# A first token mixer whose pool and convolution groups are normalised, turned and multiplied out ahead of its gating group

## The reference

```python
def token_mixer(h, w_in, pool_w, pool_scale, sgu_ln_g, sgu_ln_b, sgu_w, sgu_b, conv_w, group_g, w_out):
    p = h @ w_in                                   # 1024 -> 2048 columns
    a, u, v, gb, gc, xc = jnp.split(p, list(SPLITS), axis=-1)   # 256, 512, 512, 256, 256, 256
    y_a = pool_mixer(a, pool_w, pool_scale)        # running means over 2, 4, 8, 16 tokens, a small product, a scale
    y_b = sgu_mixer(u, v, sgu_ln_g, sgu_ln_b, sgu_w, sgu_b)     # u * (w_s @ layernorm(v) + b)
    y_c = short_conv_mixer(gb, gc, xc, conv_w)     # gb * conv3(gc * xc)
    y = jnp.concatenate([
        rmsnorm(y_a, group_g[:D_POOL]),
        rmsnorm(y_b, group_g[D_POOL:D_POOL + D_SGU]),
        rmsnorm(y_c, group_g[D_POOL + D_SGU:]),
    ], axis=-1)
    return y @ w_out

for l in range(2):                                 # first block
    x = x + token_mixer(rmsnorm(x, norm1_g[l]), ...)
    x = x + (swiglu(...) if l == 0 else moe_ffn(...))
```

## Time and profile before

| | |
|---|---|
| median of 3 runs | 2629.82 us (2627.33 to 2630.14) |
| the profiled execution | 2627.75 us |
| its span | 2626.0 us |
| granted TensorE clock, mean | 0.958 |
| PE busy | 2480.6 us (94%) |
| DVE busy | 1898.3 us (72%) |
| ACT busy | 1453.6 us (55%) |
| first mix1 stage, pieces begin / last rows begin | 37.21 / 121.93 us |
| second mix1 stage, pieces begin | 374.24 us |

### The profile page before, as it was taken

How to read it: one execution, slowest core, us unless ns; L and a number is a source line. 1 busy time by engine, 2 the same in 40 slices (tenths; PEclk the granted TensorE clock), 3 DMA queues, 4 the chain that set the end, 5 groups by cost and what they waited for, 6 DMA issues and landing times.

```text
span 2626.0 us, 39723 instructions
## 1 busy us (share of the span) xinstructions
PE 2480.6 (94%) x14992; PEld 2200.3 (84%) x14992; DVE 1898.3 (72%) x2061; ACT 1453.6 (55%) x1598; POOL 25.8 (1%) x47
## 2 busy tenths in 40 slices
PE   5799998799999999999999979998999999989998
PEld 5788887799999999999999968886788788867887
DVE  4676666588888888888888876668476676684665
ACT  3354443476767676767676754444444544544543
POOL 3000000000000000000000000000000000000000
PEclk8999999799999999999999989998799999996999
DMA  5455543398989898989898955542255555431552
GB/s 194 147 182 182 189 161 129 121 359 325 360 324 360 323 362 323 359 326 359 326 359 326 359 196 191 183 144 102 81 179 190 177 183 187 155 119 51 181 186 95
DMA packets 83809, 594.35 MB, mean 226 GB/s; under 512 B 9861, under 2 KB 10183, under 8 KB 12567
## 3 DMA queue, kind: packets, MB, share of 16 engines
q1 hardware_dynamic: 81216, 587.76, 62.5%
q0 software_dynamic: 1936, 4.44, 0.5%
q10 hardware_dynamic: 582, 1.16, 0.1%
HBM read 592.27 MB, written 1.05 MB: 226 GB/s over the span
## 4 chain that ended last, share of the span: by engine, by line
PE 87%; DVE 8%; ACT 2%; issue 1%; DMA 1%; ACTq 0%; DVEq 0%
PE banks L911 16%; PE banks L964 9%; PE banks L966 8%; PE banks L900 8%; PE banks L970 8%; PE banks L901 8%; PE banks L902 8%; PE banks L913 8%; DVE lo L1463 2%; PE banks L1187 2%; PE banks L940 2%; PE banks L1067 1%; DVE xhl L1540 1%; PE banks L998 1%; DMA stage_rows<-in_sgu_b 1%
## 5 line engine op out<-in xcount | busy, mean ns | idle before, releaser
L1463 DVE TENSOR_TENSOR lo<-raw,hi 128x2048 fp32r<-128x2048 f32 x550 | 1254.6, 2289 | 273.0 <-ACT hi L507 272.1
L507 ACT CAST hi<-raw 128x2048 fp32r<-128x2048 f32 x550 | 1049.8, 1909 | 232.3 <-PE banks L970 125.7
L911 PE MATMUL banks<-xhl,hi 128*128 128x512 f32 x1776 | 629.1, 398 | 1.2 <-DVE gsum L1494 1.2
L900 PE MATMUL banks<-hi,xhl 128*128 128x256 f32 x1952 | 566.7, 290 | 10.1 <-DVE xhl L1540 7.6
L901 PE MATMUL banks<-lo,xhl 128*128 128x256 f32 x1952 | 554.8, 284 | 0.0
L902 PE MATMUL banks<-hi,xhl 128*128 128x256 f32 x1952 | 554.8, 284 | 0.0
L913 PE MATMUL banks<-xhl,lo 128*128 128x256 f32 x1776 | 498.5, 281 | 0.0
L911 PEld LDWEIGHTS banks<-xhl,hi 128*128 128x128 f32 x1776 | 333.6, 188 | 83.7 <-DVE lo L1463 1.6
L900 PEld LDWEIGHTS banks<-hi,xhl 128*128 128x128 f32 x1952 | 376.2, 193 | 22.6 <-issue 15.7
L901 PEld LDWEIGHTS banks<-lo,xhl 128*128 128x128 f32 x1952 | 376.9, 193 | 2.6
L902 PEld LDWEIGHTS banks<-hi,xhl 128*128 128x128 f32 x1952 | 376.3, 193 | 0.0
(11 more groups left out here) (346 smaller groups left out, 2415.1 us busy)
## 6 DMA issues: line engine op xcount, KB each, us to landing
raw<-in_moe_w_gate SPq DMA_DIRECT2D x112, 1024.0 KB, 4.9
raw<-in_moe_w_up SPq DMA_DIRECT2D x112, 1024.0 KB, 4.9
raw<-in_moe_w_down SPq DMA_DIRECT2D x112, 1024.0 KB, 4.9
raw<-in_ffn_w_gate SPq DMA_DIRECT2D x58, 1024.0 KB, 4.8
raw<-in_ffn_w_up SPq DMA_DIRECT2D x58, 1024.0 KB, 4.8
raw<-in_ffn_w_down SPq DMA_DIRECT2D x58, 1024.0 KB, 4.8
raw<-in_mix_pieces SPq DMA_DIRECT2D x46, 1024.0 KB, 4.8
raw<-in_mix_pieces SPq DMA_DIRECT2D x2, 768.0 KB, 4.1
```

Of the source, the lines that this page charges most:

```text
L507: nc.scalar.copy(hi[:, hslot(S, c), 0:n], raw[:, c % RING, 0:n]).then_inc(S.hi_done, 1)
L900: pe.matmul(o, xh[:, x0 + k, tk], hi[:, hr, wgt], start=(first and n == 0), stop=False)
L911: pe.matmul(bank[b + s][:, :], hi[:, hr, a:a + P], xhl[:, k, :], start=(k == 0), stop=False, skip_group_check=True)
L1463: v.tensor_tensor(lo[:, c % RING, 0:n], raw[:, c % RING, 0:n], hi[:, hslot(S, c), 0:n].bitcast(F32), ALU.subtract).then_inc(S.lo_done, 1)
```

## The change

The pieces come in another order: a, gc, xc, gb, v, v, u, u, and the rows of `w_out` in the order pool, convolution, gating, gating (`MIX1_COLS`, `MIX1_ROWS`). DVE does the pool sums after `lo` B+3, the convolution after `lo` B+4, and `y1` of both groups after `lo` B+5; PE does the pool products after its third piece and the transposes of the convolution after its fourth. The norm of these two groups (the new `group_norm` and `squares`) and their four chunks (`EDGES`) go first: PE turns them after its sixth piece, and they are rounded into a new tile `yahl`. The statistics of v follow after that, then `vn`, and the gating products after the eighth piece. Then the product with the pool rows runs, then the gating chunks (`MIDDLE`) are turned, and the other three row pieces follow. PSUM banks and the columns of the small statistics tiles are dealt out anew.

```diff
-MIX1_COLS = (768, 1024, 0, 1536, 1792, 1280, 256, 512)
+MIX1_COLS = (0, 1536, 1792, 1280, 768, 1024, 256, 512)
+MIX1_ROWS = (0, 768, 256, 512)
...
+        yahl = s1("yahl", [P, 4, 2 * T], F32R)
+        yah, yal = yahl[:, :, 0:T], yahl[:, :, T:2 * T]
...
-        MIX1_BANKS = (0, 1, 6, 7, 2, 3, 4, 5)
+        MIX1_BANKS = (6, 7, 2, 3, 0, 1, 6, 7)
+        EDGES, MIDDLE = (0, 1, 6, 7), (2, 3, 4, 5)
-        Y_BANKS = (0, 1, 6, 7)
+        Y_BANKS = (4, 0, 1, 5)
... ACT
+            squares(((0, 0, DP), (2, DP + DS, D)), 1)
+            act.wait_ge(ev("y_var"), 2 * l + 1)
+            nc.scalar.activation(by_group(std)[:, :, ::2], by_group(var)[:, :, ::2], ACT.Sqrt).then_inc(ev("y_std"), 1)
+            act_hi(act, main, B + 7, 0)
+            act.wait_ge(ev("v_var"), l + 1)
+            nc.scalar.activation(std[:, 2:4], var[:, 2:4], ACT.Sqrt).then_inc(ev("v_std"), 1)
+            act_hi(act, main, B + 8, 0)
+            turned_y(lambda k: yah[:, k if k < 2 else k - 4, :], EDGES, 0)
             for i in range(2):
+                act.wait_ge(main.multiplied, B + 7 + i)
...
+            squares(((1, DP, DP + DS),), 2)
...
+            turned_y(lambda k: xh[:, k, :], MIDDLE, 2)
             act_hi(act, main, B + 11, 0)
... PE
-                if m in (2, 3, 4):
+                if m < 3:
                     pe_cols(pe, main, n, 0, bk, T).then_inc(main.multiplied, 1)
                 else:
+                    if m == 6:
+                        pe.wait_ge(ev("y_raw"), 2 * l + 1)
                     pe.wait_ge(main.lo_done, split_no(main, n) + 1)
                     pe_toks(pe, main, n, (bk, bk), FW).then_inc(main.multiplied, 1)
+                if m == 0:
+                    pe_turn_r(pe, st)
+                if m == 2:
+                    pe.wait_ge(ev("pool_in"), l + 1)
+                    pe.wait_ge(ev("poolw_in"), 64)
... (the four pool products)
+                if m == 3:
+                    pe.wait_ge(ev("conv_in"), l + 1)
... (the four transposes)
+                if m == 5:
+                    pe.wait_ge(ev("y_ready"), 2 * l + 1)
+                    pe_turn(pe, y1, Y_BANKS, EDGES, ev("y_turned"))
             pe.wait_ge(ev("vn_out"), 2 * (l + 1))
... (the eight gating products)
+            pe.wait_ge(ev("yl_out"), 8 * l + 4)
+            pe_rows(pe, main, B + 8, 0, yah[:, 0:2, :], yal[:, 0:2, :], TT, first=True)
+            pe.wait_ge(ev("y_ready"), 2 * (l + 1))
+            pe_turn(pe, y1, Y_BANKS, MIDDLE, ev("y_turned"))
+            pe_rows(pe, main, B + 9, 0, yah[:, 2:4, :], yal[:, 2:4, :], TT)
             pe.wait_ge(ev("yl_out"), 8 * (l + 1))
+            pe_rows(pe, main, B + 10, 0, xh[:, 2:4, :], xl[:, 2:4, :], TT)
+            pe_last_rows(pe, st, B + 11, xh[:, 4:6, :], xl[:, 4:6, :])
... POOL
-            pool.wait_ge(ev("y_raw"), 1)
+            pool.wait_ge(ev("y_raw"), 2)
... DVE
+                lo_piece(main, B + 2, 0)
+                lo_piece(main, B + 3, 0)
+                dve.wait_ge(main.multiplied, B + 1)
... (the pool sums, unchanged, up to pool_in)
+                lo_piece(main, B + 4, 0)
+                dve.wait_ge(main.multiplied, B + 3)
... (the convolution, unchanged, up to conv_in)
+                lo_piece(main, B + 5, 0)
... (y1 of the pool and convolution groups, then_inc y_raw)
+                lo_piece(main, B + 6, 0)
+                group_norm(((0, 0, DP), (2, DP + DS, D)), slice(0, 3, 2), 6 * l + 4, 1)
+                dve.wait_ge(main.multiplied, B + 6)
... (the statistics of v, up to v_var)
+                lo_piece(main, B + 7, 0)
... (vn, up to vn_out)
+                rest_y(lambda k: yal[:, k if k < 2 else k - 4, :], lambda k: yah[:, k if k < 2 else k - 4, :], EDGES, 0)
+                lo_piece(main, B + 8, 0)
+                lo_piece(main, B + 9, 0)
                 dve.wait_ge(ev("sgu_out"), 2 * (l + 1))
                 dve.wait_ge(ev("u_out"), 4 * (l + 1))
... (y1 of the gating group, then_inc y_raw)
+                group_norm(((1, DP, DP + DS),), 1, 6 * l + 6, 2)
+                lo_piece(main, B + 10, 0)
+                rest_y(lambda k: xl[:, k, :], lambda k: xh[:, k, :], MIDDLE, 4)
                 lo_piece(main, B + 11, 0)
```

More of the change, by code:

```diff
@@ L681, in act_mix1 @@
                 act_hi(act, main, B + m, 0)
[L682 to L687, removed]
+            act.wait_ge(main.multiplied, B + 4)
             act.wait_ge(rt_done, st["M"] + 1)
@@ L691, in act_mix1, with squares @@
                                      scale=rstd[:, t:t + 1]).then_inc(ev("gb_out"), 1)
+            act_hi(act, main, B + 6, 0)
+            def squares(groups, n):
+                act.wait_ge(ev("y_raw"), 2 * l + n)
+                for t in range(TT):
+                    for g, c0, c1 in groups:
+                        nc.scalar.activation(xn[:, t, c0:c1], y1[:, t, c0:c1], ACT.Square,
+                                             accum_out=ssq[:, 8 + 3 * t + g:9 + 3 * t + g]).then_inc(ev("y_sq"), 1)
@@ new lines, in turned_y @@
+            def turned_y(dst, chunks, n):
+                for i, k in enumerate(chunks):
+                    act.wait_ge(ev("y_turned"), 4 * l + n + i // 2 + 1)
+                    nc.scalar.activation(dst(k), bank[Y_BANKS[k // 2]][:, k % 2 * T:(k % 2 + 1) * T], ACT.Copy,
+                                         scale=col(("group", l), k)).then_inc(ev("yh_out"), 1)
+            squares(((0, 0, DP), (2, DP + DS, D)), 1)
+            act.wait_ge(ev("y_var"), 2 * l + 1)
+            nc.scalar.activation(by_group(std)[:, :, ::2], by_group(var)[:, :, ::2], ACT.Sqrt).then_inc(ev("y_std"), 1)
@@ L704, in act_mix1 @@
[L704 to L708, removed]
+                act_hi(act, main, B + 9 + i, 0)
+            squares(((1, DP, DP + DS),), 2)
+            act.wait_ge(ev("y_var"), 2 * l + 2)
@@ L1143, in pe_mix1 @@
                 n, bk = B + m, MIX1_BANKS[m]
[L1144 to L1147, removed]
-                if m in (2, 3, 4):
+                if m < 3:
                     pe_cols(pe, main, n, 0, bk, T).then_inc(main.multiplied, 1)
                 else:
+                    if m == 6:
+                        pe.wait_ge(ev("y_raw"), 2 * l + 1)
                     pe.wait_ge(main.lo_done, split_no(main, n) + 1)
                     pe_toks(pe, main, n, (bk, bk), FW).then_inc(main.multiplied, 1)
+                if m == 0:
[3 more added lines that the diff above has]
+                    pe.wait_ge(ev("poolw_in"), 64)
+                    for t in range(TT):
+                        for c in range(2):
+                            mm = pe.matmul(bank[6][:, t * 256 + c * P:t * 256 + c * P + P], dT[:, c, t * P:t * P + P],
+                                           poolw[:, l, c, :], start=True, stop=True)
+                    mm.then_inc(ev("pool_out"), 1)
+                if m == 3:
+                    pe.wait_ge(ev("conv_in"), l + 1)
+                    for t in range(TT):
+                        for c in range(2):
+                            mm = pe.transpose(bank[7][:, t * 256 + c * P:t * 256 + c * P + P],
+                                              zc[:, c, t * P:t * P + P], ident[:, :])
+                    mm.then_inc(ev("conv_out"), 1)
+                if m == 5:
+                    pe.wait_ge(ev("y_ready"), 2 * l + 1)
+                    pe_turn(pe, y1, Y_BANKS, EDGES, ev("y_turned"))
             pe.wait_ge(ev("vn_out"), 2 * (l + 1))
@@ L1685, in mix1 @@
                 mark(ev("conv_in"))
[L1686 to L1694, removed]
+                lo_piece(main, B + 5, 0)
+                if l == 0:
+                    dve.wait_ge(ev("small_in"), 16 * N_SMALL)
+                else:
+                    dve.wait_ge(ev("small1_in"), 48)
                 dve.wait_ge(ev("pool_out"), l + 1)
@@ L1702, in mix1 @@
                 ins.then_inc(ev("y_raw"), 1)
[L1703 to L1709, removed]
-                link(v.reciprocal(rstd[:, 2:8], std[:, 2:8]))
@@ new lines, in mix1, with group_norm @@
+                sums, vars_ = by_group(ssq), by_group(var)
+                def group_norm(groups, own, squares, n):
+                    dve.wait_ge(ev("y_sq"), squares)
+                    for g, c0, c1 in groups:
+                        ins = v.tensor_scalar(vars_[:, :, g], sums[:, :, g], 1.0 / (c1 - c0), EPS, ALU.mult, ALU.add)
+                    ins.then_inc(ev("y_var"), 1)
+                    dve.wait_ge(ev("y_std"), 2 * l + n)
+                    link(v.reciprocal(by_group(rstd)[:, :, own], by_group(std)[:, :, own]))
+                    for t in range(TT):
+                        for g, c0, c1 in groups:
+                            ins = v.tensor_scalar(y1[:, t, c0:c1], y1[:, t, c0:c1],
+                                                  rstd[:, 8 + 3 * t + g:9 + 3 * t + g], None, ALU.mult)
+                    ins.then_inc(ev("y_ready"), 1)
@@ new lines, in mix1 @@
+                for t in range(TT):
+                    for b in range(2):
```

(25 more changed lines are left out.)

94 lines of the change are left out of this document (19 added, 75 removed).

## The result

The changed kernel takes 2600.27 us (median of 4 runs, 2598.87 to 2601.27) against 2629.98 us in the same session (2627.33 to 2630.64). The ratio is 0.9887, with a 95% interval of 0.9872 to 0.9903: 29.7 us, 1.1% faster. Forecast were 2602.5 and a range of 2596 to 2611. A second session gave 2601.09 against 2630.27, ratio 0.9885 (0.9869 to 0.9902). Between the two profiled executions the difference is smaller, 26.5 us.

What follows compares the result with a forecast made beforehand. PE was taken as the bound, with only idle time and clock to gain. Time without a piece falls from 19.65 to 6.0 us a stage, 27.2 in all, giving 2602.5 us, range 2596 to 2611.

Steps and rivals of the forecast that it cites:

- The bound: PE, busy 94% of the span; with no matmul removed, only its idle time and the clock could yield a gain.
- Time without a piece: Time per stage when PE multiplies no input or row piece: from 19.65 us to 6.0.
- the prediction's bill: PE's time between input and row pieces before the change, listed as products, transposes and idle time: 19.65 us in total.
- the sum: Gain of 13.6 us a stage, 27.2 over both, taken from the kernel before.
- PE's small groups: Work on PE between pieces: pool products 0.90, convolution transposes 0.45, gating products 1.78, eight transposes 0.9 us.
- The 1.1 us of idle time: PE's remaining wait before turning the gating chunks: DVE's chain of 20.8 us against PE's work of 19.7.
- The waits of the first phase: PE's waits for `pool_in`, `conv_in` and the first `y_ready`, with slack of 0.2, 0.7 and 4.6 us.
- DVE's chain: Work from the end of the sixth piece to the scaled gating group, 20.8 us, which PE must wait for.
- Rival 1, the clock: Clock falls at the new pause in one or both stages: 3 to 7.8 us back, 2605.5 to 2610; chance 0.14.
- the step by which I set the rule of the Trainium skill aside: Transposes keep the clock up, read from its rise around 103 us; so nothing taken for the 7.8 us.
- Rivals 2 to 4: Gain part lost to new waits (2610, 0.08); half clock between input pieces (2640, 0.02); hole hidden otherwise (2629.8, 0.02).

Runs made afterwards that it cites:

- second run of the changed kernel: The changed kernel itself, unaltered, run once more on the chip of the later variants: 2601.09 us.
- the experiment with three additions: Changed kernel with three unused 128x512 additions on DVE ahead of the gating `y1` in each stage: 2604.69 us.
- the moved `lo` pieces: Kernel before, with `lo` B+9 moved behind `y1` and `lo` B+10 behind the scaling on DVE: 2627.38 us against 2630.27.
- the single norm: Changed kernel with one norm for all three groups at the end, all 16 transposes together and the row pieces behind them: 2616.70 us.
- the split row piece: Changed kernel with the second turn in the middle of row piece B+9 instead of ahead of it: 2597.25 us.
- the row piece behind the turn: Changed kernel with the pool rows (piece B+8) multiplied behind the turn of the gating chunks, not ahead of it: 2614.58 us.

## Why the prediction was right

**The bound.** What the change could gain stood at one place of each stage, as the prediction says, and nearly all of it was gained. Time without a piece in the first stage: forecast 6.0, measured 0.81 + 0.36 + 0.79 + 1.71 + 0.86 + 0.85 = 5.4, from the starts in the timeline above. Of the 14.3 us that went there, 12.0 are idle time (10.85 and 1.84, now 0.69) and 2.0 the sixteen transposes, which no longer run at half clock. (The single terms of the prediction's bill add up to 19.50; its total of 19.65 is taken from starts and is right.)

**The terms of the sum.** Each of PE's small groups was 0.05 to 0.11 us cheaper than I took it. The 1.1 us of idle time was 0.86. Against that stand two terms that I did not have, 0.4 each: the three row pieces take 16.8 us, not 16.45 (5.67, then 11.16 for two), 0.3 of it because the two that read the new tile `yahl` run slower (last section), and the input pieces up to the gating product 49.0, not 48.6, because after each group between them the next matmul starts 0.08 later, and the first piece ran 0.2 longer. So the first stage gained 13.49 against 13.6.

**The second stage** gained 15.07. 1.4 of the 1.5 above the sum lie in its first piece: it ran at half clock until 380.3 before and until 363.9 after, that is for 6.1 and 2.9 us. The second run of the changed kernel shows that the change has no part in it: there the piece was at half clock for 6.15 us, as before, and the stage took 75.59, a gain of 13.63 us against 13.6 forecast. The window of that first piece, in the second run's trace (columns as in the earlier trace rows):

```profile
361.30:367.45 6.15, 6.15 (x29) 6.15 (x30) 2.87 (x6) 3.05 (x5) 0.00 (x0) 0.50 0.00 0
```

Startup and what comes after the mixers gave back 2.1 (0.28 and 1.8), which leaves 26.5 in the span, 0.7 less than forecast. The medians differ by more, 29.7 us, and the four runs of the changed kernel fall in two pairs: 2598.87 and 2599.28 with a mean granted clock of 0.968, 2601.25 and 2601.27 with 0.963. That the median came out 2.2 us below the forecast is of this size: luck with the clock and not a term of the sum.

**The waits of the first phase** were reckoned at 0.2, 0.7 and 4.6 us of slack, and none showed. Measured from the end of DVE's work to the end of PE's piece, it was 0.3, 0.9 and 5.0. Moving one `lo` piece ahead of the pool sums turned the 0.2 into 4.5 us of idle time and 11.8 us of time, so these were the right places to watch.

**DVE's chain** is what binds now: 20.6 us measured for 20.8, and the experiment with three additions gives 2.16 us for 2.13.

**Rival 1, the clock.** It did not fall; nor did it after a pause of 2.85 us before the same transposes; with 4.53 among the pieces, and with 6.28 and 7.21 before the turn, it did. But the step by which I set the rule of the Trainium skill aside was weaker than I wrote. I read from the kernel before that sixteen transposes had raised the clock, so transposes count. With the moved `lo` pieces the same sixteen transposes ran from 97.35, with the same pause behind them, and the clock did not rise until 108.8, six microseconds into the rows, and in the second stage 3.2 us into them. After the single norm's sixteen, it rose at 100.8, 0.6 us into the rows. That transposes alone can be followed by a rise stands (the kernel before, both stages); that they reliably bring it does not. What the Trainium skill states in "TensorE: Matmul & The Clock Gate", Part 4: PE-mode transpose, that transposes don't count as busy for the clock, is contradicted by the first and agrees with the second, and what decides between them stays open. For the sum it made no difference: behind a pause of 0.86 us the clock stayed at 1.00 in both stages, and in the variant with 2.85 us too.

**Rivals 2 to 4.** No gain was lost in a new wait beyond the 0.86; no half clock among the pieces; nothing else had hidden the hole.

## What to carry to other kernels

Look for independent groups that share one norm, one turn and one product: finish those whose inputs come first, so that their share of the product stands ready for the pause which the last group's chain makes. The early norm by itself gave 0.65 us of the stage, and 8.3 with the row piece under the chain: what pays is matrix work placed where PE would wait. And a shorter pause is worth its length only if the clock agrees: 1.87 us less of it bought nothing in one stage of the kernel before, as the rows then began at half clock, and 0.4 us in the other.

## What the runs showed of the hardware that was not expected

The row matmuls run at two paces at full clock. The timeline of PE in the changed kernel around 104 us:

```profile
103.70 0.40 PE L982 MATMUL banks<-hi,xhl 128*128 128x512 f32 x1
103.94 0.39 PE L984 MATMUL banks<-lo,xhl 128*128 128x512 f32 x1
...
104.85 0.39 PE L984 MATMUL banks<-lo,xhl 128*128 128x512 f32 x1
105.08 0.39 PE L982 MATMUL banks<-hi,xhl 128*128 128x512 f32 x1
```

From start to start it is 0.233 us a matmul within the row pieces from 90.49 to 104.2, and 0.227 from 104.6 on, the granted clock being 1.00 in both. DVE's activity does not explain it: DVE is idle from 103.1 to 105.4, across the change, and busy again at the faster pace. Nor do the transfers: there were 86 GB/s from 103 to 104, at the slower pace, and 442 from 106 to 107, at the faster. The step goes with the place in PE's work. The row pieces whose activations lie in the new tile `yahl` run at 0.233 throughout, and the first six matmuls of the first piece that reads `xhl` are slow too; the seventh and all behind it are fast. That is so in the first stage of the changed kernel (`xhl` from 103.24), of the split row piece (101.64), of the row piece behind the turn (110.96) and of the single norm (111.79), and the kernel before, all of whose row pieces read `xhl`, is at 0.227 from 106.74, its sixth row matmul. So about 0.3 us of a stage come with the new tile (48 matmuls at 0.006). Whether it is where the tile lies or something else in these pieces was not tested.
